# Where the copy of product 1, the third sum's rounding and the sum of products 1 and 6 stand in the first pair of each feed-forward stage

## The reference

```python
def _swiglu(x, w_in, w_out):
    gate, up = jnp.split(x @ w_in, 2, axis=-1)
    return (jax.nn.silu(gate) * up) @ w_out

x = x + 0.5 * _swiglu(_rmsnorm(x, n1_g[l]), ffn1_w_in[l], ffn1_w_out[l])
```

## Time and profile before

| | |
|---|---|
| median of 3 runs | 2025.08 us (2025.03 to 2025.24) |
| profiled execution, its own time | 2024.85 us |
| span of the profiled execution | 2022.8 us |
| PE | busy 2006.3 us, 99% of the span, 12322 matmuls |
| PEld | busy 1764.4 us, 87% |
| DVE | busy 1255.4 us, 62% |
| ACT | busy 1063.8 us, 53% |
| POOL | busy 1114.4 us, 55% |
| TensorE clock granted | 1.00 of full speed |
| first product of each feed-forward's first pair | at 51.5, 754.0, 1098.1 and 1693.3 us |

### The profile page before, as it was taken

How to read it: one execution, slowest core, us unless ns; L and a number is a source line. 1 busy time by engine, 2 the same in 40 slices (tenths; PEclk the granted TensorE clock), 3 DMA queues, 4 the chain that set the end, 5 groups by cost and what they waited for, 6 DMA issues and landing times. The chain is left out here.

```text
span 2022.8 us, 33284 instructions
## 1 busy us (share of the span) xinstructions
PE 2006.3 (99%) x12322; PEld 1764.4 (87%) x12322; DVE 1255.4 (62%) x2245; ACT 1063.8 (53%) x1764; POOL 1114.4 (55%) x936
## 2 busy tenths in 40 slices
PE   9999999999999999999999999999999999999999
PEld 7998998777778889989987998998878878998997
DVE  7752765667762477626768753665688868742762
ACT  7642654344443456525656652554677766642651
POOL 2764775433333447746764765675323346764763
PEclk9999999999999999999999999999999999999999
DMA  4232323422221323332232333223344432332332
GB/s 171 95 110 89 113 95 117 138 84 64 72 74 52 100 79 114 110 109 84 95 109 79 115 104 105 94 92 121 114 131 128 128 106 78 110 107 84 112 95 96
DMA packets 69087, 206.19 MB, mean 102 GB/s; under 512 B 8448, under 2 KB 9472, under 8 KB 68928
## 3 DMA queue, kind: packets, MB, share of 16 engines
q1 hardware_dynamic: 67520, 201.29, 31.5%
q10 hardware_dynamic: 1408, 2.78, 0.4%
HBM read 189.49 MB, written 2.10 MB: 95 GB/s over the span
## 5 line engine op out<-in xcount | busy, mean ns | idle before, releaser
L624 POOL TENSOR_TENSOR w_lo<-raw,w_hi 128x512 fp32r<-128x512 f32 (+2 forms) x464 | 519.8, 1146 | 636.4 <-ACT w_hi L1255 474.7
L1255 ACT ACTIVATE w_hi<-raw 128x512 fp32r<-128x512 f32 (+2 forms) x472 | 359.0, 765 | 320.8 <-PE ps L701 253.9
L636 POOL TENSOR_TENSOR w_lo<-s,w_hi 128x512 fp32r<-128x512 f32 x234 | 303.1, 1297 | 199.2 <-ACT w_hi L1255 197.5
L777 PE MATMUL ps<-t_hi,w_hi 128*128 128x256 f32 x1248 | 353.6, 283 | 7.0 <-DVE scratch L1954 4.0
L778 PE MATMUL ps<-t_lo,w_hi 128*128 128x256 f32 x1248 | 353.2, 283 | 0.0
L779 PE MATMUL ps<-t_hi,w_lo 128*128 128x256 f32 x1248 | 353.2, 283 | 0.0
L636 POOL TENSOR_TENSOR w_lo<-raw,w_hi 128x512 fp32r<-128x512 f32 x234 | 302.3, 1305 | 58.0 <-ACT w_hi L1255 58.0
L777 PE MATMUL ps<-xn_hi,w_hi 128*128 128x256 f32 x936 | 265.3, 283 | 3.4 <-ACT scratch L1255 3.3
L778 PE MATMUL ps<-xn_lo,w_hi 128*128 128x256 f32 x936 | 264.9, 283 | 0.0
L779 PE MATMUL ps<-xn_hi,w_lo 128*128 128x256 f32 x936 | 264.9, 283 | 0.0
L699 PE MATMUL ps<-xn_hi,w_hi 128*128 128x512 f32 x648 | 258.7, 399 | 0.0
(11 more groups left out here) (259 smaller groups left out, 3738.5 us busy)
## 6 DMA issues: line engine op xcount, KB each, us to landing
raw<-weights SPq DMA_DIRECT2D x294, 512.0 KB, 3.3
raw<-weights SPq DMA_DIRECT2D x68, 256.0 KB, 2.8
raw<-weights SPq DMA_DIRECT2D x32, 384.0 KB, 3.1
k_hi_twice<-sb_k_hi SPq DMA_DIRECT2D x31, 128.0 KB, 2.3
k_lo_twice<-sb_k_lo SPq DMA_DIRECT2D x31, 128.0 KB, 2.3
x_sb<-x_t SPq DMA_DIRECT2D x8, 256.0 KB, 6.1
bias<-rel ACTq DMA_DIRECT2D x1, 2048.0 KB, 9.0
q_both<-sb_q_hi SPq DMA_DIRECT2D x16, 128.0 KB, 2.2
```

What stands on the lines that cost most here:

```text
L624: last = nc.gpsimd.tensor_tensor(w_lo[s][:, k, :], raw[s][:, k, :], w_hi[s][:, k, :].bitcast(F32), ALU.subtract)
L636: nc.gpsimd.tensor_tensor(quad_of(n, i, w_lo), factor(n, F, i, raw, s_sum), quad_of(n, i, w_hi).bitcast(F32), ALU.subtract).then_inc(S["q_ ...
L777: pe.matmul(to, w[0][:, k, :], hi, start=opens, stop=False, skip_group_check=True)
L1255: return nc.scalar.activation(dst, src, ACT.Copy)
```

## The change

In the first pair of each feed-forward stage (c = 0, F = `PLAIN[n]`):

- `copy_p1` and `round_7(n, F, 7)` move on ACT from the head of `up_in_seven` into `plain_tiles`. `round_7(…, 7)` now stands ahead of `silu` of the last plain pair, and `copy_p1` ahead of (feed-forward 0) or behind (the others) that `silu`, and in all of them ahead of the last plain pair's `round_h`.
- `copy_p1` of the first two pairs no longer waits for `h_made`.
- In feed-forwards 1 to 3 the load of ACT's silu table is written out ahead of `copy_c`; it was put in ahead of `silu(n, 0)`, behind `copy_c`. The number of table loads stays 13.
- `add_p6` of the pair moves on DVE from behind `sum_3(F+1)` to the head of the cycle, ahead of `sum_4`.

```diff
         def copy_p1(n, F):
             act.wait_ge(S["p1_done"], PAIR[n, F] + 1)
-            act.wait_ge(S["h_made"], FT * n + F - 1)
+            if F >= PLAIN[n] + 2:
+                act.wait_ge(S["h_made"], FT * n + F - 1)
             copy(up_of[F % 2][:, HALVES[0]], PS[:, P1_BANK, HALVES[0]]).then_inc(S["p1_copied"], 1)
...
                 round_7(0, PLAIN[0], 2)
+                round_7(0, PLAIN[0], 7)
+                copy_p1(0, PLAIN[0])
                 silu(0, 3)
                 round_h(0, 3)
...
             round_7(n, F, 1)
+            act.preload_act_table_set("silu_and_others")
             copy_c(n, F)
             silu(n, 0)
...
             round_7(n, F, 2)
+            round_7(n, F, 7)
             silu(n, 1)
+            copy_p1(n, F)
             round_h(n, 1)
...
-                copy_p1(n, F)
-                round_7(n, F, 7)
+                if F > first or c:
+                    copy_p1(n, F)
+                    round_7(n, F, 7)
...
             more, late = F + 1 < end, F > first
+            opens = not late and c == 0
+            if opens:
+                add_p6(n, F)
             if late:
                 add_p7_p5(n, F - 1)
...
-            add_p6(n, F)
+            if not opens:
+                add_p6(n, F)
             if more:
                 sum_2(n, F + 1)
             gate_first(n, F)
```

## The result

The changed kernel takes **2028.91 us** (median of 21 runs, 2027.17 to 2030.53) against 2024.89 for the kernel before (21 runs beside them, 2024.23 to 2025.57). The ratio is 1.0018, 95% interval 1.0012 to 1.0024: slower by 4.0 us, just within 0.2%, though the interval reaches past it. The forecast was 2025.9 with a range to 2028.2. The case within 0.2% came true by its number, but the time lies 0.7 us above the range.

A forecast was written before the change was run, and what follows sets the result against it. PE's list was the path: what counts is when product 1 of each second pair starts. -0.73 - 0.64 + 1.85 + 0.29 = +0.8 us on 2024.85 gives 2025.6, with the median's 0.23 2025.9; range 2023.0 to 2028.2.

The forecast's parts named there:

- The case within 0.2%: Whole kernel: time changes by no more than 0.2% (4 us), too little to tell from no change; chance 0.87.
- What PE waits for: First pairs: no copy wait, 0.5 us or so for `add_p6`, `gate_first` waits of 2.2 us (1.6 in feed-forward 1).
- The 3.48 us: First pairs: product 1 of the second pair starts no sooner than 3.48 us behind `sum_1(F+1)`, in all four feed-forwards.
- Rival (a): First pairs: `gate_first` is in time and PE goes on behind product 7; -8.6 us, 2016.5 us; chance 0.08.
- The four terms: Shift of the second pair's product 1 in feed-forwards 0 to 3: +0.29, +1.85, -0.64, -0.73 us.
- The table load: ACT, feed-forwards 2 and 3: the 1.28 us load hides in idle time ahead of `copy_c`; chain gains 0.92 and 1.01.
- rival (c): Table load holds ACT up to twice its 1.28 us in feed-forwards 2 and 3; +3.1 us, 2028.2; chance 0.04.
- rival (b): Clock falls to 1.2 GHz behind PE's single waits in feed-forwards 0, 2, 3; 5.1 us more, 2030.2; chance 0.05.

## Why the prediction was wrong

**What PE waits for: right.** No wait for the copy, 0.55 or so for `add_p6`, and four waits for `gate_first` of 2.23, 1.62, 2.23 and 2.23 (forecast 2.2 and 1.6). The 3.48 us from `sum_1(F+1)` to product 1' held in all four; in feed-forward 3, `sum_1` at 1705.28 gives 1708.76, and product 1' starts at 1708.74. Rival (a) is out.

**The four terms: right, one of them off by 0.3.** Forecast +0.29, +1.85, -0.64, -0.73; measured without the falls +0.27, +1.86, -0.35, -0.67, which is +1.1 for +0.8. The one that is off is feed-forward 2, where in the profiled execution `copy_c` started 0.21 behind the end of the load instead of 0.02; with only 2 and 3 changed `copy_c` followed the load by 0.01 and the stage gave -0.58. The kernel with filled waits gives the whole: 2025.92 for a forecast of 2025.9.

**The table load: right.** It is hidden where it stands in 2 and 3, and rival (c) is out. The timeline of ACT in feed-forward 3 of the changed kernel:

```profile
1694.14 0.62 ACT L1255 ACTIVATE w_hi<-raw 128x512 fp32r<-128x512 f32 x1
1694.78 1.28 ACT L1460 ACT_TABLE_LOAD   x1
1696.30 0.60 ACT L1255 ACTIVATE ps<-raw 128x512 f32<-128x512 f32 x1 [0.24 <-DVE scratch L1808]
1696.84 0.62 ACT L1403 ACTIVATE scratch<-scratch 128x512 f32<-128x512 f32 x1
```

The load ends at 1696.06, and `copy_c` then waits 0.24 for DVE, not for the table. The Trainium skill gives a drain of about 1380 ns beside each load (page "ScalarE: Activation LUTs", section "What ACT_TABLE_LOAD costs"); were it behind the load, `copy_c` could by this estimate not have started before 1697.4. The trace does not bear it out, and ahead of the load there is no room for it either: it starts 0.02 behind the end of the row before it.

**The step that failed is the one against rival (b):** "Against: every row is at 1.00", and its chance of 0.05. The mechanism, the three places and the price were written down, 1.44 us for a product at the lower clock and 2030.2 for all three. The rows of the changed kernel measured 1.31 and 1.43 a fall, and the slowest two runs lie at 2029.79 and 2030.53. What was wrong is the evidence on which this term was left at nothing in the sum. The row at 1.00 behind the 2.00 us wait was one execution, in which the clock happened to stay up; two of the next three executions of the same kernel had it at 0.50 in the same place. And a fall there costs the kernel before nothing, so that its even times said nothing against it either. With about two falls in the median run, the missing term was some 2 x 1.4 = 2.8 us: 2025.9 + 2.8 = 2028.7 for a measured 2028.91.

**Why the change makes it dearer.** Before, PE's one wait of 2.0 us stood in front of product 5 of feed-forward 2, with waits of 1.05 and 1.32 in front of products 2 and 7 behind it that take up a delay. The change gathers the waits in front of product 1', as three of 2.2 us, and behind that PE runs through. So the same fall now moves everything to the end of the kernel. By the steps there were 7 + 24 + 6 = 37 falls behind 63 such waits in the 21 runs, about as often as the 30 runs at 0.999 in 56 of before. The Trainium skill describes such a loss (page "TensorE: Matmul & The Clock Gate", section "HAM oscillation — how this bites in real kernels"): a burst of matmuls that follows a stall starts on the lower clock. The traces of the changed kernel agree, with matmuls at 0.21 us for 0.12 from the first one behind a wait of 2.2 us; in the kernel before the burst ran at 0.12 for another 0.5 and 1.3 us first. The page's stalls were longer than these and had a fall each; here it came behind some and not others.

**What stays open** is what decides in a given run whether, and when, the clock falls. Waits of 1.8 to 2.2 us had a fall in some executions and none in others. The wait of 1.6 showed no step of 1.4 us in 11 runs with only feed-forward 1 changed; the waits of 1.3 us and less (the load alone, the two versions with `gate_first` moved) none in 11, 7 and 6 runs, and the filled waits none in 11. These kernels differ in more than the length of one wait, and no experiment changed that alone.

## What to carry to other kernels

Here a wait that was taken away in front of one instruction came back in front of a later one, because the last thing that the path waits for had not moved: `gate_first`, which stood behind sums that it does not need, and moving it ahead of two of them, and leaving feed-forward 1 alone, turned +4.0 us into -5.5. On an engine that takes its list in order, put an instruction whose input comes late behind those whose inputs are there (`add_p6` in feed-forward 1 cost 1.86 us by standing first). And do not read the clock from one execution: look at several, price a fall by what PE has behind it (here nothing where long enough waits followed, 1.3 to 1.4 us where none did), and try filling a long wait that cannot be removed; breaking it by one product did not help here.

## What the runs showed of the hardware

- Round PE waits of 2.0 to 2.2 us the granted clock fell to 0.50 in some executions and not in others of the same kernel, from 0.4 us ahead of the wait's end to 1.3 us behind it; the low stretch was mostly about 3.4 us (62.3 to 65.7 in the changed kernel, 1102.2 to 1105.6 in the kernel before) and cost 1.3 to 1.4 us where no wait follows.
- A wait of 2.2 us broken by a product into 1.8 and 1.0 did not prevent it: 10 of 11 runs were below 1.000, and in one place the low stretch was 6.8 us. 2.28 us of matmuls on a constant, in place of the wait, did, in 11 of 11 runs.
- A mean clock of 0.999 or 0.998 over 2025 us looks like nothing; it is one or two such stretches, and in the changed kernel each was worth as much as the forecast gain of feed-forwards 2 and 3 together, 1.37.
